# Attention scores from stacked split halves, with both layers written out, in a two-layer hybrid decoder

## What is computed

```
mq = rms_norm(split_heads(m_q), ...)      # 4 heads of width 64, 512 tokens
mk = rms_norm(split_heads(m_k), ...)
s_own = einsum('bhqd,bhtd->bhqt', mq, mk) * scale     # causal; the past block too
ck = rms_norm(split_heads(mem_kv[..., :256]), ...)    # 256 memory rows
cq = rms_norm(split_heads(c_q), ...)
s = einsum('bhsd,bhmd->bhsm', cq, ck) * 64 ** -0.5
```

## Time and profile before

| | |
|---|---|
| median of three runs | 1237.35 us (1234.19 to 1238.35) |
| the profiled execution | 1238.22 us; span 1236.5 us |
| PE busy | 1135.5 us (92%) |
| DVE busy | 895.5 us (72%) |
| ACT busy | 698.5 us (56%) |
| POOL busy | 163.4 us (13%) |
| mean granted TensorE clock | 0.954 |

### The profile page before, as it was taken

How to read it: one execution, slowest core, us unless ns; L and a number is a source line. 1 busy time by engine, 2 the same in 40 slices (tenths; PEclk the granted TensorE clock), 3 DMA queues, 4 the chain that set the end, 5 groups by cost and what they waited for, 6 DMA issues and landing times.

```text
span 1236.5 us, 18265 instructions
## 1 busy us (share of the span) xinstructions
PE 1135.5 (92%) x5538; PEld 921.4 (75%) x5538; DVE 895.5 (72%) x1288; ACT 698.5 (56%) x970; POOL 163.4 (13%) x238
## 2 busy tenths in 40 slices
PE   4999999999999999999279999999999999999990
PEld 3887677788788888887258876777887888888870
DVE  5467655737999999998194665557489999999973
ACT  6322423414888888887252223234248988888860
POOL 3005001000111110111400050010010111111111
PEclk9999899988999999999679998999989999999995
DMA  9622200206999979997943222102079998999965
GB/s 341 190 86 68 69 19 33 86 34 236 343 382 375 379 255 385 377 383 301 344 142 105 71 65 69 35 18 103 35 276 377 374 384 297 325 379 388 380 249 216
DMA packets 121892, 277.46 MB, mean 224 GB/s; under 512 B 13265, under 2 KB 13473, under 8 KB 121680
## 3 DMA queue, kind: packets, MB, share of 16 engines
q1 hardware_dynamic: 106912, 240.30, 53.6%
q0 software_dynamic: 14896, 36.19, 8.2%
HBM read 269.56 MB, written 23.07 MB: 237 GB/s over the span
## 4 chain that ended last, share of the span: by engine, by line
PE 82%; DVE 9%; issue 3%; ACT 3%; DMA 2%; POOL 0%; ACTq 0%; POOLq 0%; DVEq 0%
PE bank L1395 22%; PE bank L1397 22%; PE bank L1396 22%; PE bank L1427 2%; PE bank L1726 2%; PE bank L1499 2%; PE bank L1520 1%; PE bank L1526 1%; PE bank L1745 1%; PE bank L1630 1%; PE bank L1494 1%; DMA hd<-pair_rows 1%; PE bank L1584 1%; DVE hd L1014 1%; DVE x L933 1%
## 5 line engine op out<-in xcount | busy, mean ns | idle before, releaser
L387 DVE TENSOR_TENSOR w_lo<-stage,w_hi 128x1024 fp32r<-128x1024 f32 x244 | 293.6, 1219 | 11.7 <-ACT w_hi L382 3.4
L382 ACT ACTIVATE w_hi<-stage 128x1024 fp32r<-128x1024 f32 x236 | 246.3, 1059 | 44.6 <-PE bank L1397 40.5
L1395 PE MATMUL bank<-w_hi,hT_hi 128*128 128x512 f32 x384 | 157.1, 409 | 3.7 <-DVE hT_lo L947 3.7
L1396 PE MATMUL bank<-w_lo,hT_hi 128*128 128x512 f32 x384 | 152.1, 396 | 0.0
L1397 PE MATMUL bank<-w_hi,hT_lo 128*128 128x512 f32 x384 | 152.0, 396 | 0.0
L387 DVE TENSOR_TENSOR more_lo<-stage,more_hi 128x1024 fp32r<-128x1024 f32 x124 | 146.1, 1217 | 2.3 <-ACT more_hi L382 1.7
L382 ACT ACTIVATE more_hi<-stage 128x1024 fp32r<-128x1024 f32 x124 | 127.9, 1061 | 14.7 <-PE bank L1397 13.0
L350 ACT ACTIVATE w_hi<-stage 128x1024 fp32r<-128x1024 f32 x56 | 58.8, 1057 | 101.0 <-PE bank L1397 101.0
L391 DVE TENSOR_TENSOR w_lo<-stage,w_hi 128x1024 fp32r<-128x1024 f32 x56 | 67.8, 1220 | 64.0 <-ACT w_hi L350 62.8
L1395 PE MATMUL bank<-w_hi,xgT_hi 128*128 128x512 f32 x264 | 104.0, 394 | 1.2 <-DVE xgT_lo L1291 1.2
L1397 PE MATMUL bank<-w_hi,xgT_lo 128*128 128x512 f32 x264 | 103.7, 393 | 0.0
(11 more groups left out here) (240 smaller groups left out, 2026.3 us busy)
## 6 DMA issues: line engine op xcount, KB each, us to landing
stage<-in_w_exp_up SPq DMA_DIRECT2D x124, 512.0 KB, 6.9
stage<-in_w_exp_gate SPq DMA_DIRECT2D x122, 512.0 KB, 6.9
stage<-in_w_exp_down SPq DMA_DIRECT2D x122, 512.0 KB, 6.7
stage<-in_w_in SPq DMA_DIRECT2D x40, 512.0 KB, 4.6
stage<-in_w_out SPq DMA_DIRECT2D x16, 512.0 KB, 3.8
stage<-in_w_mem_kv SPq DMA_DIRECT2D x8, 512.0 KB, 9.0
h_scratch<-act POOLq DMA_DIRECT2D x8, 512.0 KB, 2.9
act<-pair_rows POOLq DMA_DIRECT2D x8, 512.0 KB, 6.4
```

Source lines behind the costliest of these rows:

```text
L382: eng.activation(x_hi[n % NX], src, ACT.Copy).then_inc(s_hi, 1)
L387: eng.tensor_tensor(x_lo[n % NX], src, x_hi[n % NX].bitcast(f32), ALU.subtract).then_inc(s_lo, 1)
L1395: pe.matmul(dst, l_hi, r_hi, start=start, stop=False)
L1396: pe.matmul(dst, l_hi, r_lo, start=False, stop=False)
```

## The change

- **Scores.** Of each head, a tile of 128 rows holds the queries' high half in the head's own 64 rows and the low half in the other 64 (`mq_both`, `cq_both`). Two more hold the keys' high half twice, one above the other, and the low half twice (`mk_hi`, `mk_lo`, `ck_hi`, `ck_lo`). A score product is two float32r matmuls over 128 rows, into the same bank.
- **Making them.** Seven banks, as before, but each takes 2 or 4 copies of 64 rows on ACT (`heads_hi`) and as many subtractions on DVE (`heads_lo`): 20 and 20 a layer, in place of 7 DVE copies.
- **Order on PE.** Chunk 3 is turned ahead of the six fills, the memory keys after two of them, `cq` after a third. `s_qn` counts chunk 3's heads too.
- **POOL.** Rotary waits for the eighth score (`s_s` 8) and uses other scratch; `kd`, the load of `g_ret` and that of the second norm's gain wait for the last (`s_s` 24). The gate waits for `g_ret`. `tile_out(2)` waits for the rotary turn.
- **Layers.** `Fori(0, DEPTH)` and the tests on the layer become Python's loop and tests. The two copies of the expert pass become the body of one loop, `Fori(0, rounds)`, whose count is 1 until the pass has read it, with a short `If(r > 0)` at its head. The wait for `s_known` ahead of that reading is now one for `s_rounds`.

Core of the diff (the change of the loops is shown for POOL, and is alike on the other engines):

```diff
+            sb("stacks_below", [128, 2, NT, CH], scope=part)
+            pq4_r = sb("proj4_r", [128, NT, CH], f32r, scope=part)
+            mk_hi = sb("mk_hi", [128, H, SEQ], f32r, scope=part)
+            mq_both = sb("mq_both", [128, H, SEQ], f32r, scope=part)
+            mk_lo3 = sb("mk_lo3", [128, 3, SEQ], f32r, scope=part)
...
-        rot_a, rot_b = act[:, 0, 0:512], act[:, 1, 0:512]
+        rot_a, rot_b = act[:, 2, 512:1024], act[:, 3, 512:1024]
+        cq_both = [act_r[:, h, 0:512].rearrange("p (t c) -> p t c", t=NT) for h in range(2)] +             [pq4_r[:, :, 256:384], pq4_r[:, :, 384:512]]
+        mk_lo = [mk_lo3[:, h, :] for h in range(3)] + [act_r[:, 3, 0:512]]
+        ck_lo = [act_r[:, 2, 0:512].rearrange("p (g c) -> p g c", g=2), ck_lo1]
...
-            with pool.Fori(0, DEPTH) as layer:
+            for layer in range(DEPTH):
...
-                pool.dma_start(g_ret[:, :], row(a["ret_norm_g"].rearrange("l h v -> l (h v)"))).then_inc(s_small, 16)
...
-                pool.wait_ge(s_hm, 2)
-                pool.dma_start(gvec[:, :], row(a["norm2_g"])).then_inc(s_gain[2], 16)
                 pool.wait_ge(s_pev, 12)
                 pool.wait_ge(s_tr, 12)
+                pool.wait_ge(s_s, 8)
...
                 pool.sem_inc(s_rot, 1)
+                pool.wait_ge(s_s, 24)
+                pool.dma_start(g_ret[:, :], row(a["ret_norm_g"].rearrange("l h v -> l (h v)"))).then_inc(s_gain[3], 16)
                 for t in range(2):
                     pool.tensor_tensor(kd[:, t, :].rearrange("p (h c) -> p h c", h=H),
                                        pq[0][:, t, 256:512].rearrange("p (h c) -> p h c", h=H),
                                        bc(kdec[:, t, :].unsqueeze(2), [128, H, DH]), ALU.mult).then_inc(s_kd, 1)
-
-
+                pool.dma_start(gvec[:, :], row(a["norm2_g"])).then_inc(s_gain[2], 16)
+                pool.wait_ge(s_gain[3], layer * 16 + 16)
...
+                pool.reg_mov(rounds, 1)
+                with pool.Fori(0, rounds) as r:
...
-                rounds = experts(True)
-                with pool.If(rounds > 1):
-                    with pool.Fori(1, rounds) as r:
-                        experts(False)
-                with pool.Else():
-                    pool.nop()
...
+                def heads_hi(j, copies):
+                    sc.wait_ge(s_tq, j + 1)
+                    for dst, src in copies:
+                        ins = sc.activation(dst, src, ACT.Copy)
+                    ins.then_inc(s_tqh, 1)
+                half = [slice(0, 64), slice(64, 128)]
+                for g in range(2):
+                    heads_hi(g, [(mq_both[half[i], 2 * g + i, :], bank[g][half[i], :]) for i in range(2)])
+                sc.wait_ge(s_tq, 4)
+                for g in range(2):
+                    heads_hi(2 + g, [(mk_hi[half[d], 2 * g + i, :], bank[2 + g][half[i], :])
+                                     for i in range(2) for d in range(2)])
+                heads_hi(4, [(ck_hi[half[d], i::2, :], bank[0][half[i], :].rearrange("p (g c) -> p g c", g=2))
+                             for i in range(2) for d in range(2)])
+                sc.wait_ge(s_tq, 7)
+                for g in range(2):
+                    heads_hi(5 + g, [(cq_both[2 * g + i][half[i], :, :],
+                                      bank[1 + g][half[i], :].rearrange("p (t c) -> p t c", t=NT)) for i in range(2)])
...
+                        dv.sem_inc(s_qn, 1)
...
-                heads_out(0, 0, ckT[:, :, :].rearrange("p g c -> p (g c)"))
-                for j in range(1, 7):
-                    heads_out(j, j % 4, hd[:, (j - 1) // 2, (j - 1) % 2, :])
...
+                def heads_lo(j, parts):
+                    dv.wait_ge(s_tqh, j + 1)
+                    for dst, src, hi in parts:
+                        ins = dv.tensor_tensor(dst, src, hi.bitcast(f32), ALU.subtract)
+                    ins.then_inc(s_tqe, 1)
+                for g in range(2):
+                    heads_lo(g, [(mq_both[half[1 - i], 2 * g + i, :], bank[g][half[i], :],
+                                  mq_both[half[i], 2 * g + i, :]) for i in range(2)])
+                for g in range(2):
+                    heads_lo(2 + g, [(mk_lo[2 * g + i][half[d], :], bank[2 + g][half[i], :],
+                                      mk_hi[half[i], 2 * g + i, :]) for i in range(2) for d in range(2)])
+                heads_lo(4, [(ck_lo[i][half[d], :, :], bank[0][half[i], :].rearrange("p (g c) -> p g c", g=2),
+                              ck_hi[half[i], i::2, :]) for i in range(2) for d in range(2)])
+                for g in range(2):
+                    heads_lo(5 + g, [(cq_both[2 * g + i][half[1 - i], :, :],
+                                      bank[1 + g][half[i], :].rearrange("p (t c) -> p t c", t=NT),
+                                      cq_both[2 * g + i][half[i], :, :]) for i in range(2)])
...
+                    if t == 2:
+                        dv.wait_ge(s_rot, 1)
...
-                for g in range(4, 4 + FILL_FIRST):
-                    fill(g)
                 pe.wait_ge(s_pev, 12)
                 pe.wait_ge(s_qn, 1)
+                for j in range(4):
+                    turn(lambda q: pq[3][:, q, 128 * j:128 * j + 128], j, s_tq)
+                for g in (4, 5):
+                    fill(g)
+                pe.wait_ge(s_qn, 2)
+                pe.wait_ge(s_tqe, 1)
                 for g in range(2):
                     for t in range(2):
                         ins = pe.transpose(bank[0][:, 256 * g + 128 * t:256 * g + 128 * t + 128],
                                            ck[:, t, 128 * g:128 * g + 128], ident)
                 ins.then_inc(s_tq, 1)
-                for j in range(1, 7):
-                    src, off = ((pq[4], 256), (pq[3], 0), (pq[3], 256))[(j - 1) // 2]
-                    if j >= 4:
-                        pe.wait_ge(s_tqe, j - 3)
-                    turn(lambda q: src[:, q, off + 128 * ((j - 1) % 2):off + 128 * ((j - 1) % 2) + 128],
-                         j % 4, s_tq)
+                fill(6)
+                for j in range(2):
+                    pe.wait_ge(s_tqe, j + 2)
+                    turn(lambda q: pq[4][:, q, 256 + 128 * j:256 + 128 * j + 128], 1 + j, s_tq)
+                for g in range(7, 4 + FILL_FIRST):
+                    fill(g)
                 pe.wait_ge(s_tqe, 7)
...
-                            part_ = slice(64 * q, 64 * q + 64)
-                            ins = pe.matmul(bank[j % 2][:, 256 * g:256 * g + 256], hd[part_, 0, g, tok],
-                                            ckT[part_, g, :], start=True, stop=True)
+                            both, out_ = cq_both[2 * g + q][:, t, :], bank[j % 2][:, 256 * g:256 * g + 256]
+                            pe.matmul(out_, both, ck_hi[:, 2 * g + q, :], start=True, stop=False)
+                            ins = pe.matmul(out_, both, ck_lo[q][:, g, :], start=False, stop=True)
                     else:
-                        h = q - 2
-                        part_ = slice(64 * (h % 2), 64 * (h % 2) + 64)
-                        ins = pe.matmul(bank[j % 2][:, 0:128 * (t + 1)], hd[part_, 1, h // 2, tok],
-                                        hd[part_, 2, h // 2, 0:128 * (t + 1)], start=True, stop=True)
+                        h, w = q - 2, 128 * (t + 1)
+                        pe.matmul(bank[j % 2][:, 0:w], mq_both[:, h, tok], mk_hi[:, h, 0:w], start=True, stop=False)
+                        ins = pe.matmul(bank[j % 2][:, 0:w], mq_both[:, h, tok], mk_lo[h][:, 0:w],
+                                        start=False, stop=True)
```

More of the change, by code:

```diff
@@ L479, in _ @@
                     load(base, n, of(a["w_mem_kv"], 256 * n, 0))
-                with sp.If(layer < 1):
+                if layer == 0:
                     for t in range(NT):
@@ L682, in _ @@
             per_unit = 16 // NS
+            rounds = sc.alloc_register("act_rounds")
             def ring():
                 return sc.snap(loaded, min_val=0, max_val=per_unit * DEPTH * (U_ATT + NT * U_PASS))
-            with sc.Fori(0, DEPTH) as layer:
+            for layer in range(DEPTH):
                 p = sc.snap(passes, min_val=0, max_val=NT * DEPTH)
@@ L818, in _ @@
                 sc.activation(warm[:, :], eps, ACT.Copy)
-                def experts(first):
+                sc.reg_mov(rounds, 1)
+                with sc.Fori(0, rounds) as r:
                     p2 = sc.snap(passes, min_val=0, max_val=NT * DEPTH)
@@ L823, in experts @@
                     sc.sem_inc(s_ye, 1)
-                    if not first:
+                    with sc.If(r > 0):
                         for n in range(NW):
                             expert_hi(sc, base_p, n)
+                    with sc.Else():
+                        sc.nop()
                     def rows_hi(i, count):
@@ L903, in experts @@
                     hidden_hi(E_N)
-                    if first:
-                        sc.wait_ge(s_known, 1)
-                        rounds = rounds_of(sc)
```

(48 more changed lines are left out.)

127 lines of the change are left out of this document (65 added, 62 removed).

## The result

The changed kernel took 1204.04 us (median of four runs, 1203.54 to 1207.51) against 1237.85 (1234.19 to 1238.61) on the same chip (also four, the profiled execution among them): ratio 0.974, 95% interval 0.971 to 0.977. The forecast was 1216, from 1207 to 1229. The direction was right; the gain was 34 us, where 21.6 were summed. The profiled span fell from 1236.5 to 1201.9, by 34.6 us.

The account below looks back on a forecast made before the run. PE, carrying 82% of the chain, was taken to bound the kernel. Attention less heads, 2 x (6.6 - 1.0) = 11.2, plus 10.4 at the turn made 21.6 us saved: 1216 us, range 1207 to 1229.

Parts of the forecast that it names:

- With 0.2 us and 0.46 us per 1000 columns: Scores in attention: price of a float32r group, fixed term kept, giving 0.67 us for a memory step.
- the second pass gone: Scores in attention: float32r takes one pass of the columns instead of two, saving 7.2 us a layer.
- the second tile: Attention steps 6 to 9, waiting for ACT: their share of the scores' saving, 1.2 us, counted for half.
- Making the heads: Start of each layer, ahead of the first scores: earlier normalising against more copies and subtractions, cost 1.0 us a layer.
- Rotary's contention: Making the heads: with POOL's rotary turn moved, DVE's normalising runs at 0.46 us each and ends 6.4 us earlier.
- POOL's moved steps: Attention and after: rotary, near 142 to 158.5, and the later loads, kd and gate all stay hidden, costing nothing.
- The turn: Between the layers: ACT's two jumps go, it starts 10.9 us earlier, 0.5 is lost to the gain's load; 10.4 us won.
- the rival's 10.8 us a layer: Clock rival, attention: TensorE at half clock for 21 us more of each layer takes the whole gain back; 6%.
- the dips go as that rival had it: Rival: clock dips vanish at the second layer's first scores and both second tiles, some 3 us each, 1207; 8%.
- Short float32r products: Rival, scores: float32r matmuls under 512 columns cost 0.23 us, so scores give nothing, 1229, or 1222 halfway; 12%.
- the lower bound I took: Scores: short float32r matmuls priced near the value products' 0.105 us (0.12 for 256 columns), not 0.23.

Follow-up runs that it names:

- the run over 64 rows: The changed kernel with each float32r score matmul over only the head's own 64 rows, queries' low half left out: 1227.6 us, ratio 0.993.
- The run with two copies of the pass: The kernel before with both layers written out but the two copies of the expert pass kept: 1227.67 us, ratio 0.995.
- the split evacuation: The changed kernel with POOL doubling the keys' low rows, ACT's four evacuations made two and two, weight split later: 1193.09 us, ratio 0.967.

## Why the prediction was too high

**The step that failed is "With 0.2 us and 0.46 us per 1000 columns".** The fit over rows 3 was right, 0.2 fixed and 0.83 per 1000 columns. What I read into it wasn't: I took the fixed term for a cost of any group and kept it. The float32r rows I leaned on give no hint, since all fills and transposes are of 128 rows. The runs showed in its place that a group of float32r products over 128 rows has no fixed term (0.48 us for four of 256 columns), and that the transposes behind it give back 0.15 us, which the prediction had at nothing: together 8.2 us a layer. Term by term, a layer:

- the second pass gone: 8 x 0.38 in memory steps (0.86 less 0.48) and 0.39 in the widest causal ones, so about 3.0 + 4 x (0.1 + 0.2 + 0.3 + 0.39) = 7.0. Forecast 7.2. Right.
- the change of rows gone: 24 x (0.19 + 0.15) = 8.2, which the run over 64 rows bears out (8.7 and 7.8). Forecast 0. The 0.15 stood in rows of the kernel before that I never set beside each other: four transposes behind scores 0.59 us, the last four, with no scores ahead, 0.44.
- the second tile: PE's waits went from 1.46 to 3.32 us (3.08 in the second layer), 1.9 lost; I had counted half of 1.2.

7.0 + 8.2 - 1.9 = 13.3, where the windows give 12.2 and 12.9. The table's 10.5 and 14.8 differ from these by clock: the kernel before lost 5.0 and 8.3 us to it, the changed one 7.2 and 6.2.

**Making the heads** was right in kind. Rotary's contention was worth 6.4 us from the start of the normalising (forecast 6.4) by the run with it back. DVE's pieces were mis-sized by 0.61 to 0.70, 20 x 0.09 = 1.8 us, since they alternate between halves. With the 1.0 forecast that is the 2.8 found in both layers, 21.4 for 18.6. The table's +1.5 and +3.2 hold besides what lies ahead of the normalising, in code that wasn't changed: 1.4 less in the first layer, 0.4 more in the second. The run with two copies of the pass, whose heads are made as before, has 1.5 less there in the first layer too, so this isn't the change's; where it comes from stays open.

**POOL's moved steps** cost nothing, as written: rotary at 142 to 158, the gate ready 14.8 us ahead, as far ahead as in the kernel before (its last part ended at 209.9, its use was at 224.6).

**The turn** gave 10.8 for 10.4 (10.2 in the second profile of the changed kernel), by the steps named: both jumps gone, the gain's load next in line. ACT's own path gave more, 12.4 us from its last copies of expert rows to its root, since the first of its two table loads (1.28 us, at 610.91) is gone too; but then DVE waited 1.8 us for the gain, where I had 0.5. The two-copies run shows that the forward jump was the smaller matter, 2.73 us and hidden.

**The rivals.** The clock took part of it back, far less than the rival's 10.8 us a layer: losses in the attentions went from 5.0 and 8.3 us to 7.2 and 6.2. At the first scores of the first layer a half-clock stretch came that wasn't there before, at 122.6 to 129.4, and this is the place that the rival named. Nor did the dips go as that rival had it: the one in the second tile is as long as before, 10.2 us at 0.50 in each layer of both kernels; the one at the second layer's first scores halved, from 6.8 us to 3.4. Rows 2 showed 3 us of the former, and I took that for the whole. Some went elsewhere: 4.8 us less behind the first attention, 1.6 more behind the second. Short float32r products cost 0.12 at 256 columns and 0.06 at 128, so that rival fell with the lower bound I took.

Over the whole: 2 x 6 more in the attentions (12.1), 2.7 less in the heads, 0.4 in the turn, 3.2 of clock elsewhere, sum 13.0, which is 34.6 less 21.6. The range ended at 1207 because it held no case in which a term of the sum was too small but for the clock's.

## What to carry to other kernels

When a group of matmuls shows a fixed term, ask what it follows and what follows it: on this chip a few products over 64 rows between products over 128 cost 0.2 us ahead and 0.15 us behind, and stacking two halves into 128 rows buys both back. Pieces on DVE or ACT that take turns between partition halves cost 0.08 us each more than pieces that stay in one; ordering them by half should save it, an estimate that no run here tested. Read a segment as length times granted clock before explaining it: here 5 us that looked like a gain in untouched code, and what the split evacuation won and lost, were clock. And look in the kernel as it is for the same instructions with another neighbour: the last transposes, with no scores ahead, were 0.15 us shorter than the others before anything was changed.

## What was not expected of the hardware

- The change from 128 rows to 64 and back: 0.19 to 0.20 and 0.15 us, whatever the type of the products.
- ACT pays for a change of half between instructions as DVE does: 0.60 against 0.51 us for 512 columns.
- A jump forward past a copy of the pass cost ACT 2.73 us in one layout of the code and 4.59 in another; only the jump back cost 6.34.
- The granted clock fell at the same places, within 0.3 us, in two executions of one kernel, but for one stretch that cost 1.7 us.
